# A two-block transformer on one core: the router's gate rows, count products, memsets and weight splits in another order

## The chip, the cores and the metric

The kernel runs on 1 core of one Trainium2 chip. The time is device microseconds from start to end of one execution; the figure for the kernel before is the median of 3 runs. The core has TensorE (PE, matrix products; PEld is its weight load), VectorE (DVE), ScalarE (ACT), GpSimd (POOL) and SyncE (SP, which here issues the weight loads). Each engine works through its own queue in order, and the queues wait for each other by semaphores.

## The reference

A block with feed-forward, recurrent, local and memory attention layers comes first; then two layers (0 and 1) of a second block. Each of these ends in a mixture of 16 experts for 256 tokens of width 1024. The change touches only this part:

```python
h = rmsnorm(x, norm2_g[l]) * (1.0 + sc2) + sh2
x = x + g2 * grouped_moe(h, w_router, router_bias, w_gate[l], w_up[l], w_down[l])
# grouped_moe: scores = sigmoid(t @ w_router); one group of 4 experts of 4 groups is chosen,
# in it the best 2 experts; their scores, normalised, weigh silu(t @ w_gate) * (t @ w_up) @ w_down
```

The modulation g2 (a row of 1024 numbers) multiplies the sum of the experts, and is needed on every partition.

## The kernel before, in words

All matrix products are made in three parts: a value is split into a high part and a low part (value minus high), and high x high, low x high and high x low are summed in PSUM (`PARTS`). For a weight tile (128 x 2048 numbers in a slot of a ring of 6 slots, loaded by SyncE) ScalarE makes the high part in two halves (`hi`, `split`, L706), and VectorE the low part, `w_lo`, in two halves (`lo`, `split`, L1928 and L1862). A tile's slot is loaded anew when TensorE has counted the tile as used.

Around the change a layer goes so. TensorE makes the products of the output projection, tiles w_out0 to w_out3 (L1111), and between them `gate_rows` (L1396): a product of a matrix of ones with the diagonal matrix of a modulation row, which puts the row on all partitions. VectorE makes the diagonal (`gate_diag`, L2050) and copies the result from PSUM (`gate_copy`, L2056). VectorE adds the projection to x (L2035, L2038), and the norm follows (L571 and L1782 to L1785). TensorE transposes the normed rows (`turn`, L1062), ScalarE and VectorE scale them on the way out of PSUM (L591, L1805). Then come a second `gate_rows`, for g2, the router's products (L1705), the sigmoid (L1035), and the selection on VectorE (L2509 to L2545), small steps of 0.2 us. Five products (L1712 to L1716) count for each expert the tokens ahead of each token, with `member`, the 0/1 matrix of the choice: the matrix `before` counts within a block of 128 tokens, `ones` gives the sum of a block. From the counts VectorE works out each token's slot and the matrix `pick` (L2561, L2564).

If every expert has at most 128 tokens, the branch `sparse` runs on every engine. TensorE gathers: 8 blocks k of 128 features for 512 slots, each into a PSUM bank (L1251, `gather`). ScalarE (L713, L715) and VectorE (L1935, L1936) turn each into a high and a low part, `xg_parts` (`expert_inputs`); semaphore `xg_act` counts ScalarE's, `xg_lo` VectorE's. Even blocks have their full value written by VectorE, odd ones by ScalarE. The columns behind slot 512 are set to 0 (L1987). Expert 0 then goes through its four tiles u0, g0, g1, u1 (up and gate, first and second half of the features; L1269); `weights` is a product that brings the slots' weights into a column of bank 4 (L1279), copied by VectorE (L1942). Behind u1 the slot numbers are spread over partitions (`spread`, L1324), and from expert 2 a loop runs over the experts. Every order named here is written out by hand.

## Time and profile before

| | us |
|---|---|
| median of 3 runs (1848.01 to 1850.01) | 1849.73 |
| the profiled execution | 1845.74 |
| its span, first to last instruction | 1843.9 |
| TensorE busy in it | 1668.1 (90%) |
| VectorE busy | 1230.0 (67%) |
| ScalarE busy | 1009.0 (55%) |
| mean granted TensorE clock | 0.955 |

Times in the rows further down are us from the span's start. A busy share is an average over stages: TensorE is full in the products, and idle in stretches such as the router's. The granted clock is 1.00 at TensorE's higher level (2.4 GHz) and 0.50 at its lower one (1.2 GHz).

### The profile page before, as it was taken

The numbers are of one execution on the slowest core, as the hardware profiler recorded it, in microseconds if no ns is written. First come the engines' busy times: TensorE is split into PE (matmuls) and PEld (weight loads), VectorE is DVE, ScalarE is ACT, GpSimd is POOL, SyncE is SP. The second block draws the span as 40 slices with busy tenths as digits, with TensorE's granted clock in tenths as the row PEclk, the third lists the DMA queues.
The fourth block names the chain that finished last, engine by engine and source line by source line (L and its number), as shares of the span: only waits on it lengthen the run. The fifth ranks groups of instructions, "written<-read, shape, count | busy, mean of one in ns | idle before, by whom it ended". The sixth has DMA issues, their size and how long they took to land.

```text
span 1843.9 us, 27068 instructions
## 1 busy us (share of the span) xinstructions
PE 1668.1 (90%) x10156; PEld 1428.9 (77%) x10156; DVE 1230.0 (67%) x1715; ACT 1009.0 (55%) x1407; POOL 27.0 (1%) x58
## 2 busy tenths in 40 slices
PE   6999997899998989876899999979897769999995
PEld 6999885488997968765688888869796657888884
DVE  5544355565546454764888888864677578888886
ACT  4444344253445433531788888844444258888884
POOL 2000000000000000001000000000000010000000
PEclk9999998999999999987899999999998879999998
DMA  8555478854554569722398998945431418898892
GB/s 261 186 188 190 144 246 269 277 167 160 183 188 145 165 207 348 274 91 92 133 331 315 333 330 313 333 144 163 137 116 68 137 63 297 320 333 319 329 333 89
DMA packets 245834, 401.86 MB, mean 218 GB/s; under 512 B 6522, under 2 KB 151596, under 8 KB 245756
## 3 DMA queue, kind: packets, MB, share of 16 engines
q1 hardware_dynamic: 244792, 398.77, 63.4%
q8 instruction: 55, 0.90, 0.2%
q0 software_dynamic: 592, 0.93, 0.2%
q10 hardware_dynamic: 372, 1.07, 0.2%
q14 instruction: 23, 0.19, 0.0%
HBM read 399.70 MB, written 1.05 MB: 217 GB/s over the span
## 4 chain that ended last, share of the span: by engine, by line
PE 80%; DVE 12%; ACT 4%; issue 2%; DMA 2%; DVEq 0%; ACTq 0%
PE bank L1269 19%; PE bank L1209 14%; PE bank L1293 10%; PE bank L1099 7%; PE bank L1222 6%; PE bank L1111 5%; PE bank L1087 5%; PE bank L1305 3%; PE bank L1136 2%; PE bank L1380 2%; DVE sb_w_lo L1862 2%; DMA sb_ring<-in_w_in 1%; PE bank L1556 1%; DVE sb_w_lo L1928 1%; PE bank L1125 1%
## 5 line engine op out<-in xcount | busy, mean ns | idle before, releaser
L1928 DVE TENSOR_TENSOR sb_w_lo<-sb_ring,sb_moe_hi 128x1024 fp32r<-128x1024 f32 x384 | 448.5, 1220 | 29.5 <-ACT sb_moe_hi L706 29.2
L706 ACT ACTIVATE sb_moe_hi<-sb_ring 128x1024 fp32r<-128x1024 f32 x384 | 381.8, 1058 | 69.2 <-PE bank L1293 33.7
L1883 DVE TENSOR_TENSOR sb_w_lo<-sb_ring,sb_w_hi 128x1024 fp32r<-128x1024 f32 x128 | 151.1, 1222 | 164.2 <-ACT sb_w_hi L661 163.9
L1209 PE MATMUL bank<-sb_hT_hi,sb_w_hi 128*128 128x256 f32 x704 | 201.3, 286 | 7.2 <-DVE sb_w_lo L1883 3.7
L661 ACT ACTIVATE sb_w_hi<-sb_ring 128x1024 fp32r<-128x1024 f32 x128 | 128.5, 1051 | 143.6 <-PE bank L1209 131.6
L1209 PE MATMUL bank<-sb_hT_lo,sb_w_hi 128*128 128x256 f32 x704 | 200.8, 285 | 0.0
L1209 PE MATMUL bank<-sb_hT_hi,sb_w_lo 128*128 128x256 f32 x704 | 200.7, 285 | 0.0
L1269 PE MATMUL bank<-sb_moe_hi,sb_xw_hi 128*128 128x512 f32 x480 | 193.6, 403 | 0.0
L1269 PE MATMUL bank<-sb_w_lo,sb_xw_hi 128*128 128x512 f32 x480 | 190.7, 397 | 0.0
L1269 PE MATMUL bank<-sb_moe_hi,sb_xw_lo 128*128 128x512 f32 x480 | 190.3, 397 | 0.0
L1862 DVE TENSOR_TENSOR sb_w_lo<-sb_ring,sb_proj_hi 128x1024 fp32r<-128x1024 f32 x100 | 117.9, 1221 | 92.0 <-ACT sb_proj_hi L641 91.9
L641 ACT ACTIVATE sb_proj_hi<-sb_ring 128x1024 fp32r<-128x1024 f32 x100 | 100.8, 1060 | 125.1 <-DMA sb_ring<-in_w_in 40.3
L1293 PE MATMUL bank<-sb_moe_hi,sb_hid_hi 128*128 128x512 f32 x512 | 145.4, 396 | 2.9 <-DVE sb_hid_hi L1954 2.9
L1209 PEld LDWEIGHTS bank<-sb_hT_hi,sb_w_hi 128*128 128x128 f32 x704 | 136.9, 194 | 8.6 <-DVE sb_w_lo L1883 4.1
L1209 PEld LDWEIGHTS bank<-sb_hT_lo,sb_w_hi 128*128 128x128 f32 x704 | 136.9, 194 | 0.7
L1209 PEld LDWEIGHTS bank<-sb_hT_hi,sb_w_lo 128*128 128x128 f32 x704 | 136.7, 194 | 0.0
L1099 PE MATMUL bank<-sb_w_lo,sb_hT_hi 128*128 128x256 f32 x480 | 136.0, 283 | 0.0
L1099 PE MATMUL bank<-sb_proj_hi,sb_hT_hi 128*128 128x256 f32 x416 | 119.8, 288 | 0.4 <-DVE sb_w_lo L1862 0.4
L1099 PE MATMUL bank<-sb_proj_hi,sb_hT_lo_l 128*128 128x256 f32 x416 | 117.9, 283 | 0.0
L1293 PEld LDWEIGHTS bank<-sb_moe_hi,sb_hid_hi 128*128 128x128 f32 x512 | 93.8, 188 | 21.3 <-DVE sb_hid_hi L1954 3.4
L1269 PEld LDWEIGHTS bank<-sb_moe_hi,sb_xw_lo 128*128 128x128 f32 x480 | 91.1, 190 | 21.7
L1269 PEld LDWEIGHTS bank<-sb_w_lo,sb_xw_hi 128*128 128x128 f32 x480 | 91.4, 190 | 20.0
(488 smaller groups left out, 3186.5 us busy)
## 6 DMA issues: line engine op xcount, KB each, us to landing
sb_ring<-in_w_up SPq DMA_DIRECT2D x64, 1024.0 KB, 5.3
sb_ring<-in_w_gate SPq DMA_DIRECT2D x64, 1024.0 KB, 5.3
sb_ring<-in_w_down SPq DMA_DIRECT2D x64, 1024.0 KB, 4.9
sb_ring<-in_ada_w SPq DMA_DIRECT2D x48, 1024.0 KB, 7.5
sb_ring<-in_w_in SPq DMA_DIRECT2D x46, 1024.0 KB, 5.4
sb_ring<-in_ffn_w_in SPq DMA_DIRECT2D x44, 1024.0 KB, 5.1
sb_ring<-in_ffn_w_out SPq DMA_DIRECT2D x22, 1024.0 KB, 4.9
sb_ring<-in_w_out SPq DMA_DIRECT2D x12, 1024.0 KB, 5.1
```

Source lines behind the costliest of these rows:

```text
L641: A(mix_hi(name)[:, c], ring[:, pos % RING, c], ACT.Copy).then_inc(s["mix_hi"], 1)
L661: A(w_hi[:, q % 2, c], ring[:, (pos0 + q) % RING, c], ACT.Copy).then_inc(s["w_hi"], 1)
L706: A(moe_hi[:, q % 3, c], ring[:, at % RING, c], ACT.Copy).then_inc(s["moe_hi"], 1)
L1087: ins = mm(out[:, j * SEQ:(j + 1) * SEQ], w[wp][:, k, j * P:(j + 1) * P], h_parts[hp][:, k, :], start=k == 0 and m == 0 and (turned is Non ...
L1099: ins = mm(out[:, t * FB:(t + 1) * FB], h_parts[hp][:, k, t * P:(t + 1) * P], w[wp][:, k, :], start=k == 0 and m == 0, stop=k == KC - 1 an ...
L1209: ins = mm(bank[4 + 2 * p + b][:, jj * SEQ:(jj + 1) * SEQ], w[wp][:, k, jj * P:(jj + 1) * P], h_parts[hp][:, k, :], start=k == 0 and m == ...
L1222: ins = mm(acc[2 * t + half][:, :], h, w[wp][:, kk, half * 512:(half + 1) * 512], start=start and kk == 0 and m == 0, stop=stop and kk == ...
L1269: ins = mm(out[:, :], x_parts[xp][:, 4 * kh + k, 0:P], w[wp][:, k, :], start=kh == 0 and k == 0 and m == 0, stop=kh == 1 and k == 3 and m ...
L1293: ins = mm(bank[6 + half][:, :], h[hp][:, 2 * kh + kk, :], w[wp][:, kk, half * 512:(half + 1) * 512], start=kh == 0 and kk == 0 and m == 0 ...
L1862: ins = tt(w_lo[:, pos % RING, c], ring[:, pos % RING, c], mix_hi(name)[:, c].bitcast(F32), ALU.subtract)
L1883: ins = tt(w_lo[:, slot, c], ring[:, slot, c], w_hi[:, q % 2, c].bitcast(F32), ALU.subtract)
L1928: ins = tt(w_lo[:, slot, c], ring[:, slot, c], moe_hi[:, q % 3, c].bitcast(F32), ALU.subtract)
```

## The change

The computation stays the same. Per layer of the second block:

- `gate_rows` for g2 goes from behind the transposes to ahead of them, behind the projection, into banks 0 and 1 in place of 4 and 5; it waits for the first half of x, which has been read out of these banks. Its diagonal goes ahead of w_out3's split on VectorE. The router's logits go to bank 2.
- The five count products become three, of 32, 32 and 16 columns; they now wait for the gate copy.
- The two memsets of `xg_parts` go from the start of `sparse` to ahead of the wait for the scores.
- ScalarE's splits of the first two expert tiles go from the start of `sparse` to behind the sigmoid.
- The gathered blocks 0 to 7 go to banks 4, 5, 0, 1, 2, 3, 6, 7 in place of 0 to 7.
- u0 waits for 4 input blocks in place of 6, `weights(0)` goes ahead of it, and on VectorE the split of g0 comes behind input 3, then the column's copy, then inputs 4 to 7.

```diff
+        IN_BANK = [bank[n] for n in (4, 5, 0, 1, 2, 3, 6, 7)]
...
-                hi(0)
-                hi(1)
                 expert_inputs()
...
-                A(rt[:, 0, :], bank[0][:, 0:T * NE], ACT.Sigmoid).then_inc(s["scores"], 1)
+                A(rt[:, 0, :], bank[2][:, 0:T * NE], ACT.Sigmoid).then_inc(s["scores"], 1)
+                for q in range(2):
+                    at = place[f"moe.{l}"] + q
+                    act.wait_ge(ring_full[at % RING], 16 * (at // RING + 1))
+                    for half in range(2):
+                        c = slice(half * TILE // 2, (half + 1) * TILE // 2)
+                        A(moe_hi[:, q, c], ring[:, at % RING, c], ACT.Copy).then_inc(s["moe_hi"], 1)
...
-                            ins = mm(bank[k][:, :], xn_parts[hl][:, t, k * P:(k + 1) * P], pick[:, t, 0:2 * SEQ],
+                            ins = mm(IN_BANK[k][:, :], xn_parts[hl][:, t, k * P:(k + 1) * P], pick[:, t, 0:2 * SEQ],
...
                 gather()
-                pe.wait_ge(s["xg_lo"], KC * l + 6)
+                pe.wait_ge(s["xg_lo"], KC * l + 4)
+                weights(0)
                 rows("u0", 0, bank[5], 0)
-                weights(0)
                 pe.wait_ge(s["w_slot"], NE * l + 1)
...
+                pe.wait_ge(s["x"], 7 + 4 * l)
+                gate_rows(2 * l + 2, bank[0:2])
                 turn(6 + 2 * l)
                 have_hT(6 + 2 * l)
-                gate_rows(2 * l + 2)
...
-                mm(bank[1][:, 0:NE], before, member[:, 0:NE], start=True, stop=True)
-                mm(bank[1][:, NE:2 * NE], before, member[:, NE:2 * NE], start=True, stop=False)
-                mm(bank[1][:, NE:2 * NE], ones[:, :], member[:, 0:NE], start=False, stop=True)
-                mm(bank[1][:, 2 * NE:3 * NE], ones[:, :], member[:, 0:NE], start=True, stop=False)
-                mm(bank[1][:, 2 * NE:3 * NE], ones[:, :], member[:, NE:2 * NE], start=False, stop=True)\
+                pe.wait_ge(s["gbc"], 2 * l + 2)
+                twice = member[:, 0:NE].unsqueeze(1).broadcast_to([P, 2, NE])
+                mm(bank[1][:, NE:3 * NE].rearrange("p (a e) -> p a e", a=2), ones[:, :], twice, start=True, stop=False,
+                   skip_group_check=True)
+                mm(bank[1][:, 0:2 * NE], before, member, start=False, stop=False, skip_group_check=True)
+                mm(bank[1][:, 2 * NE:3 * NE], ones[:, :], member[:, NE:2 * NE], start=False, stop=True, skip_group_check=True)\
...
-                for part in xg_parts:
-                    v.memset(part[:, :, 2 * SEQ:PICKS].bitcast(F32), 0.0)
                 lo(0)
-                for k in range(5):
+                for k in range(4):
                     expert_inputs(k)
                 lo(1)
-                for k in range(5, KC):
+                weights(0)
+                for k in range(4, KC):
                     expert_inputs(k)
-                weights(0)
                 lo(2)
+                lo(3)
                 cp(sel_r[0:NE, :, :], ident[0:NE, 0:NE].unsqueeze(2).broadcast_to([NE, NE, P])).then_inc(s["posT"], 1)
-                lo(3)
...
-                gate_copy(2 * l + 1, 0.5)
+                gate_copy(2 * l + 1, 0.5, bank[4:6])
+                gate_diag(l, 40)
                 split(f"w_out3.{l}")
...
                 normalise_x()
-                gate_diag(l, 40)
...
-                gate_copy(2 * l + 2, 1.0)
+                gate_copy(2 * l + 2, 1.0, bank[0:2])
+                for part in xg_parts:
+                    v.memset(part[:, :, 2 * SEQ:PICKS].bitcast(F32), 0.0)
```

On TensorE, layer 0, from the last projection product to the last count product, before (L1062 the transposes, L1396 the gate rows, L1705 the router, L1712 to L1716 the counts; `sb_dist` holds `member`, `sb_arena` the diagonal and `before`):

```order
L1111 MATMUL bank<-sb_proj_hi,sb_hT_lo_l 128x512 x2
L1062 MATMUL bank<-sb_ident,sb_xn 128x128 x16
L1396 MATMUL bank<-sb_arena,sb_ones 128x512 x2
L1705 MATMUL bank<-sb_router,sb_hT 128x16 x16
L1712 MATMUL bank<-sb_dist,sb_arena 128x16
L1713 MATMUL bank<-sb_dist,sb_arena 128x16
L1714 MATMUL bank<-sb_dist,sb_ones 128x16
L1715 MATMUL bank<-sb_dist,sb_ones 128x16
L1716 MATMUL bank<-sb_dist,sb_ones 128x16
```

and after (L1116, L1401, L1067, L1711, L1720 to L1723 are the same steps):

```order
L1116 MATMUL bank<-sb_proj_hi,sb_hT_lo_l 128x512 x2
L1401 MATMUL bank<-sb_arena,sb_ones 128x512 x2
L1067 MATMUL bank<-sb_ident,sb_xn 128x128 x16
L1711 MATMUL bank<-sb_router,sb_hT 128x16 x16
L1720 MATMUL bank<-sb_dist,sb_ones 128x32
L1722 MATMUL bank<-sb_dist,sb_arena 128x32
L1723 MATMUL bank<-sb_dist,sb_ones 128x16
```

The gate rows have moved ahead of the transposes, and two count products are gone.

On VectorE, layer 0, the split of w_out3 and what stands around it, before (L1862 a split, L2056 the gate copy, L2035 and L2038 the addition to x):

```order
L1862 TENSOR_TENSOR sb_w_lo<-sb_ring,sb_proj_hi 128x1024 x2
L2056 TENSOR_SCALAR sb_gbc<-bank 128x512 x2
L1862 TENSOR_TENSOR sb_w_lo<-sb_ring,sb_proj_hi 128x1024 x2
L2035 TENSOR_TENSOR sb_xn<-bank,sb_gbc 128x512 x2
L2038 TENSOR_TENSOR sb_x<-sb_x,sb_xn 128x1024
```

and after (L2054 is the diagonal):

```order
L1868 TENSOR_TENSOR sb_w_lo<-sb_ring,sb_proj_hi 128x1024 x2
L2060 TENSOR_SCALAR sb_gbc<-bank 128x512 x2
L2054 TENSOR_TENSOR sb_arena<-sb_ident,sb_modc 128x1024
L1868 TENSOR_TENSOR sb_w_lo<-sb_ring,sb_proj_hi 128x1024 x2
L2039 TENSOR_TENSOR sb_xn<-bank,sb_gbc 128x512 x2
L2042 TENSOR_TENSOR sb_x<-sb_x,sb_xn 128x1024
```

The diagonal now stands between the gate copy and the split.

On VectorE at the start of `sparse`, layer 0, before (L1987 the memsets, L1928 a weight split, L1935 and L1936 the expert inputs):

```order
L1987 MEMSET sb_xg_hi 128x8x128
L1987 MEMSET sb_xg_lo 128x8x128
L1928 TENSOR_TENSOR sb_w_lo<-sb_ring,sb_moe_hi 128x1024 x2
L1935 TENSOR_SCALAR sb_arena<-bank,sb_scol,sb_modc 128x512
L1936 TENSOR_TENSOR sb_xg_lo<-sb_arena,sb_xg_hi 128x512 x2
L1935 TENSOR_SCALAR sb_arena<-bank,sb_scol,sb_modc 128x512
L1936 TENSOR_TENSOR sb_xg_lo<-sb_arena,sb_xg_hi 128x512 x2
L1935 TENSOR_SCALAR sb_arena<-bank,sb_scol,sb_modc 128x512
L1936 TENSOR_TENSOR sb_xg_lo<-sb_arena,sb_xg_hi 128x512
L1928 TENSOR_TENSOR sb_w_lo<-sb_ring,sb_moe_hi 128x1024 x2
L1936 TENSOR_TENSOR sb_xg_lo<-sb_arena,sb_xg_hi 128x512
L1935 TENSOR_SCALAR sb_arena<-bank,sb_scol,sb_modc 128x512
```

and after (L1934, L1941, L1942 are the same steps, L1948 the column's copy):

```order
L1934 TENSOR_TENSOR sb_w_lo<-sb_ring,sb_moe_hi 128x1024 x2
L1941 TENSOR_SCALAR sb_arena<-bank,sb_scol,sb_modc 128x512
L1942 TENSOR_TENSOR sb_xg_lo<-sb_arena,sb_xg_hi 128x512 x2
L1941 TENSOR_SCALAR sb_arena<-bank,sb_scol,sb_modc 128x512
L1942 TENSOR_TENSOR sb_xg_lo<-sb_arena,sb_xg_hi 128x512 x2
L1934 TENSOR_TENSOR sb_w_lo<-sb_ring,sb_moe_hi 128x1024 x2
L1948 COPY sb_by_slot<-bank 128x1
L1941 TENSOR_SCALAR sb_arena<-bank,sb_scol,sb_modc 128x512
L1942 TENSOR_TENSOR sb_xg_lo<-sb_arena,sb_xg_hi 128x512 x2
L1941 TENSOR_SCALAR sb_arena<-bank,sb_scol,sb_modc 128x512
L1942 TENSOR_TENSOR sb_xg_lo<-sb_arena,sb_xg_hi 128x512 x2
L1934 TENSOR_TENSOR sb_w_lo<-sb_ring,sb_moe_hi 128x1024 x4
```

The memsets are gone from here, and the second split and the column's copy stand ahead of the last four inputs.

## Rows read from the trace of the kernel before

**Rows 1.** Windows of layer 0: length, busy us (instructions) per engine, PEclk, DMA, GB/s.

```profile
880.00:893.00 13.00, 9.39 (x33) 7.32 (x34) 12.62 (x16) 10.57 (x15) 0.00 (x0) 0.86 0.01 1
...
940.00:960.00 20.00, 20.00 (x93) 16.39 (x92) 17.46 (x19) 16.42 (x22) 0.00 (x0) 1.00 0.92 327
```

**Rows 2.** Timeline, layer 0, norm to router: start, us, engine, line, instructions, [idle before].

```profile
838.94 2.35 DVE L1862 TENSOR_TENSOR sb_w_lo<-sb_ring,sb_proj_hi 128x1024 fp32r<-128x1024 f32 x2
...
848.01 0.61 PE L1111 MATMUL bank<-sb_proj_hi,sb_hT_lo_l 128*128 128x512 f32 x2
...
854.64 1.22 DVE L2050 TENSOR_TENSOR sb_arena<-sb_ident,sb_modc 128x1024 f32<-128x1024 f32 x1
...
855.17 3.68 PE L1062 MATMUL bank<-sb_ident,sb_xn 128*128 128x128 f32 x16 [6.55 <-ACT sb_xn L578]
...
858.04 1.90 DVE L1805 TENSOR_SCALAR sb_hT<-bank,sb_scol,sb_modc 128x256 f32<-128x256 f32 x4 [2.18 <-PE bank L1062]
...
860.04 3.52 PE L1396 MATMUL bank<-sb_arena,sb_ones 128*128 128x512 f32 x4 [1.19 <-issue]
...
863.39 3.92 PE L1705 MATMUL bank<-sb_router,sb_hT 128*128 128x16 f32 x32
...
863.59 1.29 DVE L2056 TENSOR_SCALAR sb_gbc<-bank 128x512 f32<-128x512 f32 x2 [3.66 <-PE bank L1396]
867.35 0.20 ACT L1035 ACTIVATE sb_dist<-bank 128x32 f32<-128x32 f32 x1 [5.99 <-PE bank L1705]
```

**Rows 3.** Timeline, the router of layer 1.

```profile
1476.31 1.96 PE L1396 MATMUL bank<-sb_arena,sb_ones 128*128 128x512 f32 x4 [1.59 <-issue]
...
1478.10 4.19 PE L1705 MATMUL bank<-sb_router,sb_hT 128*128 128x16 f32 x32
...
1482.33 0.20 ACT L1035 ACTIVATE sb_dist<-bank 128x32 f32<-128x32 f32 x1 [4.70 <-PE bank L1705]
```

**Rows 4.** Windows of 1 us, TensorE: length, busy us (instructions), PEclk, DMA, GB/s.

```profile
863.00:864.00 1.00, 1.00 (x8) 0.91 0.00 0
...
866.00:867.00 1.00, 1.00 (x10) 0.80 0.00 0
...
883.00:884.00 1.00, 1.00 (x5) 0.67 0.00 0
...
893.00:894.00 1.00, 1.00 (x5) 0.95 0.00 0
...
1474.00:1475.00 1.00, 0.72 (x6) 0.91 0.00 0
```

**Rows 5.** Chain of waits, layer 0: start, us, engine, tile, line, number.

```profile
873.55 0.43 PE bank L1713 x2
...
892.78 4.55 PE bank L1269 x12
...
931.58 2.80 PE bank L1269 x12
```

**Rows 6.** Timeline, layer 0, gathering and first expert.

```profile
876.56 3.90 ACT L706 ACTIVATE sb_moe_hi<-sb_ring 128x1024 fp32r<-128x1024 f32 x4 [9.01 <-DVE sb_fits L2549]
...
879.84 1.22 PE L1251 MATMUL bank<-sb_pick,sb_xn_hi 128*128 128x512 f32 x2 [4.58 <-DVE sb_pick L2564]
880.11 0.91 DVE L1987 MEMSET sb_xg_hi<- 128x1024 f32 x1 [0.16 <-issue]
...
884.34 0.77 ACT L715 ACTIVATE sb_arena<-bank,sb_modc,sb_scol 128x512 f32<-128x512 f32 x1
...
888.56 0.61 PE L1251 MATMUL bank<-sb_pick,sb_xn_lo 128*128 128x512 f32 x2
...
889.77 2.35 DVE L1928 TENSOR_TENSOR sb_w_lo<-sb_ring,sb_moe_hi 128x1024 fp32r<-128x1024 f32 x2
...
892.78 0.50 PE L1269 MATMUL bank<-sb_moe_hi,sb_xg_hi 128*128 128x512 f32 x1 [3.61 <-DVE sb_xg_lo L1936]
...
906.63 1.21 PE L1324 MATMUL bank<-sb_posT,sb_sel_r 16*128 16x256 f32 x8
```

More of the change, by code:

```diff
@@ L382, in build @@
         SLOT_COUNTS = dict(
-            act=(("xg_act", KC), ("moe_hi", 12 * NE), ("xw", 2 * NE - 2), ("m_silu", NE), ("m_hid_hi", NE), ("ye_hi", NE), ("pos_out", NE // 2)),
+            act=(("xg_act", KC), ("moe_hi", 12 * NE - 4), ("xw", 2 * NE - 2), ("m_silu", NE), ("m_hid_hi", NE), ("ye_hi", NE), ("pos_out", NE // 2)),
             pe=(("gathered", KC), ("pos_turned", 1), ("pos_bc", NE // 2), ("w_psum", NE), ("m_hidT", NE), ("scattered", NE)),
@@ L712, in expert_inputs @@
                         put_in = dict(scale=scol[:, l, 1, k:k + 1], bias=modc[:, l, 24 + k:25 + k])
-                        ins = A(xg_parts[0][:, k, 0:2 * SEQ], bank[k][:, :], ACT.Identity, **put_in)
+                        ins = A(xg_parts[0][:, k, 0:2 * SEQ], IN_BANK[k][:, :], ACT.Identity, **put_in)
                         if k % 2:
-                            ins = A(xg_full[:, k, :], bank[k][:, :], ACT.Identity, **put_in)
+                            ins = A(xg_full[:, k, :], IN_BANK[k][:, :], ACT.Identity, **put_in)
                         ins.then_inc(s["xg_act"], 1)
@@ L1390, in ada_turn, with gate_rows @@
                 ins.then_inc(s["ada_turned"], 1)
-            def gate_rows(run):
+            def gate_rows(run, out):
                 pe.wait_ge(s["diag"], run)
                 for half in range(2):
-                    ins = mm(bank[4 + half][:, :], ones[:, :], diag[:, 4 * half:4 * half + 4, :], start=True, stop=True)
+                    ins = mm(out[half][:, :], ones[:, :], diag[:, 4 * half:4 * half + 4, :], start=True, stop=True)
                 ins.then_inc(s["gate_bc"], 1)
@@ L1696, in _ @@
                         pe.wait_ge(s["mT_dve"], 4 * l + 3)
-                        gate_rows(2 * l + 1)
+                        gate_rows(2 * l + 1, bank[4:6])
+                pe.wait_ge(s["x"], 7 + 4 * l)
+                gate_rows(2 * l + 2, bank[0:2])
                 turn(6 + 2 * l)
                 have_hT(6 + 2 * l)
-                gate_rows(2 * l + 2)
                 pe.wait_ge(s["router_in"], 32)
@@ L1704, in _ @@
                     for k in range(KC):
-                        ins = mm(bank[0][:, t * NE:(t + 1) * NE], hT[:, k, t * P:(t + 1) * P], router[:, k, :],
+                        ins = mm(bank[2][:, t * NE:(t + 1) * NE], hT[:, k, t * P:(t + 1) * P], router[:, k, :],
                                  start=k == 0, stop=k == KC - 1)
@@ L1719, in _ @@
                 pe.wait_ge(s["combine"], run)
-                pe.wait_ge(s["gbc"], 2 * l + 2)
                 fits_ = pe.value_load(fits[0:1, 0:1], min_val=0, max_val=1)
@@ L1934, in expert_inputs @@
                     if k % 2 == 0:
-                        link(ts(xg_full[:, k, :], bank[k][:, :], scol[:, l, 1, k:k + 1], modc[:, l, 24 + k:25 + k], M, AD))
+                        link(ts(xg_full[:, k, :], IN_BANK[k][:, :], scol[:, l, 1, k:k + 1], modc[:, l, 24 + k:25 + k], M, AD))
                     tt(xg_parts[1][:, k, 0:2 * SEQ], xg_full[:, k, :], xg_parts[0][:, k, 0:2 * SEQ].bitcast(F32), ALU.subtract)\
@@ L2051, in gate_diag, with gate_copy @@
                    modc[:, l, c0:c0 + KC].unsqueeze(2).broadcast_to([P, KC, P]), M).then_inc(s["diag"], 1)
-            def gate_copy(run, scale):
+            def gate_copy(run, scale, src):
                 v.wait_ge(s["gate_bc"], run)
                 for half in range(2):
-                    ins = ts(gbc[:, half * 512:(half + 1) * 512], bank[4 + half][:, :], scale, None, M)
+                    ins = ts(gbc[:, half * 512:(half + 1) * 512], src[half][:, :], scale, None, M)
                 ins.then_inc(s["gbc"], 1)
```

## Prediction

> **What bounds the kernel now.** I read the windows by stage first, then the timeline of one router and the first expert behind it, then the chain of waits through the same stretch. In the steady part of the experts TensorE is busy 20.00 of 20 us at a granted clock of 1.00 while the DMA engines are at 0.92 [rows 1]; the chain there is TensorE's own products, one tile of 12 after another in 2.80 us [rows 5]. So nothing that this change touches can be gained inside that loop: it is gained or lost ahead of it, and whatever moves the start of the first expert's products moves all that follows, in both layers, since the ring of weight tiles is refilled only as TensorE releases tiles. In the 13 us around the gathering of the tokens TensorE is busy 9.39 us, at a clock of 0.86 [rows 1]. That is the place: a serial chain norm, transposes, gate rows, logits, selection on VectorE, count products, gathering, first expert. The change works on five links of it, twice (layer 0 at 850 to 907 us, layer 1 at 1466 to 1522 us).
>
> **Gate rows (PE, L1396).** Today four passes stand between the transposes and the router's products. In layer 0 they start at 860.04 and the router follows at 863.39 to 863.55, so they cost 3.52 us there [rows 2]; in layer 1 from 1476.31 to 1478.10, 1.79 us [rows 3]. The factor of two is the clock: 512 columns in two passes at half speed, against full speed. After the change they stand behind the last product of w_out3, which ends at 848.62 [rows 2], and the first half of x, finished beside it; TensorE then idles until the transposes at 855.17, 6.5 us, so 1.8 us at the full clock are hidden. Their diagonal (1.22 us on DVE, L2050 [rows 2]) must be ready and now stands ahead of the last weight split. That split ran 838.94 to 841.29; shifted by 1.22 it ends at 842.5. The 24 products that need it end at 848.62 and take 24 x 0.233 = 5.6 us (12 in 2.80 us, [rows 5]), so they start at 843.0. It is hidden by 0.5 us; without that cover it would cost the overlap, at most 1.2 us in each layer. I take 0.
>
> But the gate rows also kept TensorE at work before the router. In layer 0 the clock is low through the transposes and rises only at 863.1, at the end of the gate rows; the router's 32 passes then run at full clock and it falls at 866.6 [rows 4]. They take 867.35 - 863.55 = 3.8 us with the last three or four low [rows 2]. In layer 1 it rose at 1474.1 during the transposes [rows 4], and the router took 4.2 us (1478.10 to 1482.33, [rows 3]), its last third low. A count pass, of the same shape but for a few columns, takes 0.43 / 2 = 0.215 us at the low clock [rows 5]; 32 such are 6.85 us. So if the clock stays low for the whole router, layer 0 ends at 860.04 + 6.85 = 866.9 instead of 867.35: +0.45 us gained, and layer 1 at 1483.15 instead of 1482.33: 0.8 us lost. If it is at full speed throughout (32 x 0.107 = 3.45 us), layer 0 gains 3.8 and layer 1 2.5 us. Without the gate rows nothing but the transposes precedes the router. They raised the clock in one layer and not in the other. I take the low end in layer 0 (+0.45) and the middle, rounded down, in layer 1 (+0.3): **0.75 us for both**, bounds -0.4 and +6.3.
>
> Here a rule stands against the middle. The row first: at 1474:1475 the clock is 0.91 although only transposes ran since 1465 [rows 4]. The Trainium skill (TensorE: Matmul & The Clock Gate, Part 4: PE-mode transpose) says that work in transpose mode does not count as busy for the clock and leaves it low. This trace disagrees in layer 1 and agrees in layer 0. By the rule both routers would be slow in the changed kernel, and this term -0.4 us in place of +0.75.
>
> **Count products.** Five products of two passes each, 0.43 us a product [rows 5], become three (two of 32 columns, one of 16; loading the weights, not the columns, sets the 0.215 us). Two products less are **0.86 us in each layer**. VectorE waits for them with nothing else left (its combine row is through by then). The wait for the gate copy, moved ahead of them, is met: in the new order that copy (1.29 us, [rows 2]) stands right behind VectorE's part of the transposes, which ends at 859.95, so it is done at 861.3, 11 us early.
>
> **Memsets.** Two of 0.91 us with 0.16 us of issue, 2.1 us per layer [rows 6], stand between selection and the first split on VectorE. In their new place they run 861.3 to 863.3, behind the gate copy and before the scores, which come at 867.35 today and between 863.8 and 867.2 afterwards. Hidden; if VectorE were late by all of it, 2 us a layer. ScalarE's four splits (3.90 us, [rows 6]) move from 876.56 to right behind the sigmoid, where it waited 9 us. They gain nothing by themselves: it is free at 880.46, before the first gathered block is there. What they buy is that the first split on VectorE has its data at once.
>
> **The first expert.** I count from the first gathering product (G = 879.84 in layer 0). Today [rows 6]: VectorE memsets until 2.2, split of u0 until 4.5, inputs 0 to 4, split of g0 at 9.93 to 12.2, input 5, and TensorE starts u0 at 12.94, 3.6 us after the last gathering product ended at 9.33. While it idled the clock went low again: it falls at 893.9 [rows 4], so the tile u0 took 4.55 us, not 2.80 [rows 5]. The spreading products start at 26.8 (906.63). There are two such stretches; layer 1's reads the same, 1494.82 to 1521.62, 26.8.
> The new order, with the same durations: split of u0 0.3 to 2.6; inputs 0 to 3 follow ScalarE, whose odd block 1 lands at 884.34 + 0.77, 5.3, and 2.0 us later block 3, at 7.3; block 3's low part is done at 8.0. Split of g0 8.0 to 10.3. TensorE ends the gathering at 9.33, does the weight column (0.41) and starts u0 at 9.75, at full clock since it never stopped: to 12.55; g0 to 15.35. On VectorE: column copy at 10.5, inputs 4 to 7 (two pairs of 2.05) to 14.6, split of g1 (2.3) to 16.85. That is late: **TensorE waits 1.5 us for the g1 split**, a new wait. g1 to 19.7, transposes of the slots 0.35, u1 (its split is done at 19.15) to 22.85, against 26.8. **3.95 us per layer, 7.9 for both.** Were no new wait there it would be 5.5 a layer; were the waiting to cost a stretch at low clock again (1.7 us, the excess of 4.55 over 2.80), 2.2. The other bank order only frees banks 4 and 5 first, which the column and u0 need; it costs nothing.
>
> **The gathering's clock.** It starts low in both layers, since nothing runs ahead of it, and rose after 3.8 us in layer 0 (at 883.66, [rows 4]) and 3.2 us in layer 1. When its start moves by some 1.3 us against the changes of the clock, the low stretch can be longer; each us of it costs 0.5. I take 1 us more in each layer, **-1.0 us for both**; bounds 0 and, all 32 passes low (13.7 us in place of 9.33), -4.4 a layer.
>
> **The sum.** 0.75 + 2 x 0.86 + 7.9 - 1.0 = 9.4 us, from the profiled execution's 1845.74 us (span 1843.9 and 1.8 around it) to 1836.4. The median of the runs is 1849.73, 4.0 above the profiled one, with the same work; I take the same difference off it: 1840.4 us.
>
> **Rivals.**
> (B) The clock pays back part: both routers low (-0.4) and the gathering's low stretch 3 us longer in each layer (-3.0). 1.7 + 7.9 - 3.4 = 6.2 us, 1843.5. For it: the two places where the change takes TensorE work away just before the router. Against it: the gathering itself is unchanged.
> (C) The clock is kind: routers at full speed (+6.3), gathering as now: 1.7 + 7.9 + 6.3 = 15.9 us, 1833.8. For it: layer 1 rose in the transposes. Against it: it fell within the router in both layers, and must then rise earlier than either.
> (D) The expert's gain goes into a new wait on VectorE. The column copy now stands before inputs 4 to 7, and waits for TensorE's column product, which waits for the gathering. If the gathering stays low to its end (13.7), the copy comes at 14.1, inputs to 18.4, g1 split 20.7, u1 ends at 26.6, the 26.8 of today. Left are the counts less the routers, 1.3 us: 1848.4. Against it: both layers rose at less than half of the gathering.
> (E) Slower: the same, and the low clock goes on through u0 and g0. It decides once the low stretch outlasts the gathering by both tiles: u0 and g0 take 5.1 us each, 14.1 + 10.2 = 24.3, then g1, transposes and u1 at full clock to 30.2, that is 3.4 us later than today per layer. -6.8 + 1.7 - 0.4 = -5.5, 1855.2. In its favour is only that u0 ran low in both layers today, but that followed 3.6 us of idling; here TensorE is busy without a gap.
> That the change does nothing is covered by D: the order of every queue does differ, and the steady loop can't take the time back, since TensorE sets it.
>
> **Chances.** Forecast 0.60, B 0.17, C 0.08, D 0.10, E 0.05. A measurement of this kernel can tell about 0.2%, 3.7 us, from no change. The forecast, B and C are beyond it: faster 0.85, D within it 0.10, E slower 0.05. The range, 1834.5 to 1846, holds the forecast with its bounds (2.2 instead of 3.95 in both experts gives 1843.9; full-clock routers in one layer about 1838), B and most of C, and leaves out D and E.
>
> **What would show it.** Right: gate rows at 848.7, seen in TensorE's timeline ahead of the transposes; the router's products directly behind them, whatever their clock; six count passes in 1.5 us; no memset behind the selection; 22 to 23.5 us from the first gathering product to the spreading ones, with a wait of 1 to 2 us for VectorE's split ahead of g1 and no low stretch in u0. Wrong: a wait ahead of w_out3's products for VectorE's split; scores found waiting because of the memsets; a low clock to the end of the gathering with VectorE idle at the column copy; or a tile of the steady loop longer than the 2.80 us of today [rows 5].

## The result, and the profile after

The changed kernel takes 1838.0 us (median of 4, 1835.05 to 1838.4) against 1849.87 (median of 4, 1848.01 to 1851.66) for the kernel before: a ratio of 0.9933, interval 0.9918 to 0.9948. Run once more, five times against nine, it takes 1839.42 against 1848.67, ratio 0.9948 (0.9934 to 0.9962). The gain is 9 to 12 us, where 9.4 was forecast. The profiled execution took 1837.8 us, its span 1836.1.

The timeline of the changed kernel, layer 0, from the projection's end to the counts (answers to [rows 2, 5]; L1401 gate rows, L1067 transposes, L1711 router, L2060 gate copy, L2505 memset, L1040 the early weight split, L1720 first count product):

```profile
848.08 1.98 PE L1401 MATMUL bank<-sb_arena,sb_ones 128*128 128x512 f32 x4
...
854.64 3.68 PE L1067 MATMUL bank<-sb_ident,sb_xn 128*128 128x128 f32 x16 [4.58 <-ACT sb_xn L579]
...
859.32 1.28 DVE L2060 TENSOR_SCALAR sb_gbc<-bank 128x512 f32<-128x512 f32 x2
...
859.50 6.98 PE L1711 MATMUL bank<-sb_router,sb_hT 128*128 128x16 f32 x32 [1.19 <-issue]
...
860.76 0.91 DVE L2505 MEMSET sb_xg_hi<- 128x1024 f32 x1 [0.16 <-issue]
...
866.52 0.20 ACT L1034 ACTIVATE sb_dist<-bank 128x32 f32<-128x32 f32 x1 [5.70 <-PE bank L1711]
866.61 3.88 ACT L1040 ACTIVATE sb_moe_hi<-sb_ring 128x1024 fp32r<-128x1024 f32 x4
...
872.12 0.63 PE L1720 MATMUL bank<-sb_dist,sb_ones 128*128 128x32 f32 x2 [5.63 <-DVE sb_dist L2546]
...
873.61 0.17 DVE L2554 TENSOR_REDUCE sb_dist<-bank 128x1 f32<-128x16 f32 x1 [0.68 <-PE bank L1723]
```

The gate rows run at 848.08, 1.98 us at the high clock, with the transposes 4.58 us of idling behind them. The router's products start 1.19 us behind the transposes, as nothing is between, but their 32 passes take 6.98 us; [rows 2] had 3.92. Gate copy and memsets lie within, 3.8 us clear of the scores. VectorE waits 0.68 us for the counts (1.53 before), which end 1.49 us after they start, against 2.36. Layer 1 is the same where [rows 3] had 4.19:

```profile
1472.56 6.98 PE L1711 MATMUL bank<-sb_router,sb_hT 128*128 128x16 f32 x32 [1.19 <-issue]
...
1479.57 0.20 ACT L1034 ACTIVATE sb_dist<-bank 128x32 f32<-128x32 f32 x1 [5.70 <-PE bank L1711]
```

The gathering and the first expert, layer 0 (answers to [rows 6]; L1256 gathering, L1934 a weight split, L716 ScalarE's block 1, L1284 the column product, L1948 its copy, L1274 expert tiles, L1329 the spreading):

```profile
878.16 1.22 PE L1256 MATMUL bank<-sb_pick,sb_xn_hi 128*128 128x512 f32 x2 [4.58 <-DVE sb_pick L2570]
878.18 2.36 DVE L1934 TENSOR_TENSOR sb_w_lo<-sb_ring,sb_moe_hi 128x1024 fp32r<-128x1024 f32 x2
...
882.66 0.77 ACT L716 ACTIVATE sb_arena<-bank,sb_modc,sb_scol 128x512 f32<-128x512 f32 x1
...
887.91 0.50 PE L1284 MATMUL bank<-sb_dist,sb_pick 128*128 128x1 f32 x4
...
888.27 0.49 PE L1274 MATMUL bank<-sb_moe_hi,sb_xg_hi 128*128 128x512 f32 x1
...
888.83 0.15 DVE L1948 COPY sb_by_slot<-bank 128x1 f32<-128x1 f32 x1
...
892.99 4.62 DVE L1934 TENSOR_TENSOR sb_w_lo<-sb_ring,sb_moe_hi 128x1024 fp32r<-128x1024 f32 x4
...
895.49 0.47 PE L1274 MATMUL bank<-sb_moe_hi,sb_xg_hi 128*128 128x512 f32 x1 [1.47 <-DVE sb_w_lo L1934]
...
901.39 1.21 PE L1329 MATMUL bank<-sb_posT,sb_sel_r 16*128 16x256 f32 x8
```

u0 starts 10.1 us after the first gathering product (12.94 before), right behind the column; g1 waits 1.47 us for the split (the wait ahead of 895.49); the spreading starts after 23.2 us, against 26.8.

Windows of 1 us, TensorE alone (length, busy us, PEclk, DMA, GB/s), answers to [rows 4]:

```profile
852.00:853.00 1.00, 0.00 (x0) 0.74 0.59 242
...
865.00:866.00 1.00, 1.00 (x6) 0.50 0.00 0
882.00:883.00 1.00, 1.00 (x3) 0.50 0.08 16
883.00:884.00 1.00, 1.00 (x5) 0.90 0.00 0
888.00:889.00 1.00, 1.00 (x8) 1.00 0.00 0
...
894.00:895.00 1.00, 0.02 (x1) 1.00 1.00 410
```

The clock stays low from 852.5 through the whole router and counts until 883.2, and is then high through u0 and the wait ahead of g1, where before it fell at 893.9. In layer 1 the wait ahead of g1 is 1.79 us, also at the high clock. Behind that stands one more wait, in the chain (start, us, what):

```profile
905.19 0.96 ACT sb_moe_hi L707
...
906.17 2.36 DVE sb_w_lo L1934 x2
908.53 0.61 DVE sb_hid_hi L1960
...
909.18 0.60 PE bank L1284 x4
...
926.16 2.80 PE bank L1274 x12
```

In the kernel before, u0 of expert 1 ran low in both layers (4.54 us). In layer 0 it now runs at the high clock, but the down products still wait for VectorE, which makes the low hidden part (L1960) only behind a weight split (L1934, waiting for ScalarE): of 1.7 us gained there only 0.3 arrives. In layer 1 the clock fell behind the spreading again and that tile took 4.55 us, so nothing was gained there. The tile of the steady loop is 2.80 us as before [rows 5].

**Where the time went**, from the profiles. Each stretch is the distance of starts: first transpose to sigmoid, counts to VectorE's maximum of them, first gathering product to the first product of down in expert 1; the last column is first transpose to that product, all stages in it:

| us, layer 0 / layer 1 | to sigmoid | counts | gathering to down | whole |
|---|---|---|---|---|
| before | 12.18 / 10.89 | 2.36 / 2.35 | 35.38 / 35.38 | 60.05 / 58.76 |
| before, again | 12.19 / 12.17 | 2.35 / 2.35 | 35.36 / 35.36 | 60.05 / 60.02 |
| after | 11.88 / 11.88 | 1.49 / 1.50 | 31.49 / 31.16 | 55.01 / 54.68 |
| after, again | 11.88 / 11.88 | 1.50 / 1.50 | 31.54 / 31.13 | 55.06 / 54.66 |
| gate rows alone | 11.88 / 11.88 | 2.35 / 2.35 | 35.16 / 36.81 | 59.52 / 61.18 |
| gate rows back | 12.18 / 12.18 | 1.50 / 1.50 | 31.45 / 31.39 | 55.26 / 55.21 |
| memsets back | 11.88 / 11.88 | 1.50 / 1.50 | 31.54 / 31.89 | 55.05 / 55.42 |
| order back | 11.88 / 11.88 | 1.50 / 1.50 | 36.56 / 36.44 | 60.08 / 59.94 |

Both stretches together: 118.81 before, 109.69 after, 9.12 us less; in the second pair of profiles 120.07 and 109.72, 10.35 less.

### The profile page after: what moved, and what is told of

It reads as the page before. It is cut to its first block, busy times and chain, and to the rows that moved or that the text cites. A ratio compares the mean times of both kernels' runs of the same rounds, so it can differ in the third digit from the quotient of the medians.

```text
span 1836.1 us, 27052 instructions
## 1 busy us (share of the span) xinstructions
PE 1670.2 (91%) x10148; PEld 1430.3 (78%) x10148; DVE 1230.2 (67%) x1715; ACT 1008.8 (55%) x1407; POOL 26.8 (1%) x58
## 4 chain that ended last, share of the span: by engine, by line
PE 80%; DVE 12%; ACT 4%; issue 2%; DMA 2%; DVEq 0%; ACTq 0%
PE bank L1274 19%; PE bank L1214 14%; PE bank L1298 10%; PE bank L1104 7%; PE bank L1227 6%; PE bank L1116 5%; PE bank L1092 5%; PE bank L1310 3%; PE bank L1141 2%; PE bank L1385 2%; DVE sb_w_lo L1868 2%; DMA sb_ring<-in_w_in 1%; PE bank L1561 1%; DVE sb_w_lo L1934 1%; PE bank L1130 1%
## 5 line engine op out<-in xcount | busy, mean ns | idle before, releaser
L1934 DVE TENSOR_TENSOR sb_w_lo<-sb_ring,sb_moe_hi 128x1024 fp32r<-128x1024 f32 x384 | 448.5, 1220 | 29.5 <-ACT sb_moe_hi L707 29.2
L707 ACT ACTIVATE sb_moe_hi<-sb_ring 128x1024 fp32r<-128x1024 f32 x376 | 373.7, 1058 | 42.0 <-PE bank L1298 33.4
L1274 PE MATMUL bank<-sb_moe_hi,sb_xw_hi 128*128 128x512 f32 x480 | 192.9, 402 | 0.0
L1274 PE MATMUL bank<-sb_w_lo,sb_xw_hi 128*128 128x512 f32 x480 | 190.1, 396 | 0.0
L1274 PE MATMUL bank<-sb_moe_hi,sb_xw_lo 128*128 128x512 f32 x480 | 189.9, 396 | 0.0
L1274 PEld LDWEIGHTS bank<-sb_moe_hi,sb_xw_lo 128*128 128x128 f32 x480 | 90.8, 189 | 21.5
L1274 PEld LDWEIGHTS bank<-sb_moe_hi,sb_xw_hi 128*128 128x128 f32 x480 | 90.8, 189 | 20.2 <-issue 0.2
```

The costliest lines, as they stand in the source:

```text
L707: A(moe_hi[:, q % 3, c], ring[:, at % RING, c], ACT.Copy).then_inc(s["moe_hi"], 1)
L1274: ins = mm(out[:, :], x_parts[xp][:, 4 * kh + k, 0:P], w[wp][:, k, :], start=kh == 0 and k == 0 and m == 0, stop=kh == 1 and k == 3 and m ...
L1934: ins = tt(w_lo[:, slot, c], ring[:, slot, c], moe_hi[:, q % 3, c].bitcast(F32), ALU.subtract)
```

## The experiments

**Gate rows alone, on the kernel before.**

```diff
-                turn(6 + 2 * l)
-                have_hT(6 + 2 * l)
-                gate_rows(2 * l + 2)
+                pe.wait_ge(s["x"], 7 + 4 * l)
+                gate_rows(2 * l + 2, bank[0:2])
+                turn(6 + 2 * l)
+                have_hT(6 + 2 * l)
...
                 gate_copy(2 * l + 1, 0.5, bank[4:6])
+                gate_diag(l, 40)
```

> The kernel before with one part of the change alone: the gate rows for g2 behind the last product of w_out3, into banks 0 and 1, their diagonal ahead of w_out3's split, the logits in bank 2, the wait for the gate copy ahead of the (five) count products. Theory: the router's 32 passes then run at the low clock, and the stretch from the first transpose to the sigmoid is 11.9 us in both layers, where it was 12.2 and 10.9; no gain, 1849 to 1850.5 us. Rival, from the run with the gate rows put back, which was 3.5 us above the changed kernel although its stretches were only 0.8 us longer: the part is worth about 3.5 us by some way that these stretches don't show, 1845 to 1847 us.

Measured: 1849.53 us (11 runs) against 1849.34 (15 runs), ratio 1.0002 (0.9993 to 1.0011). The router in layer 0 (timeline, TensorE and ScalarE):

```profile
860.49 6.98 PE L1706 MATMUL bank<-sb_router,sb_hT 128*128 128x16 f32 x32 [1.19 <-issue]
...
867.50 0.20 ACT L1035 ACTIVATE sb_dist<-bank 128x32 f32<-128x32 f32 x1 [5.69 <-PE bank L1706]
```

The stretch is 11.88 us in both layers, as expected: a part that takes 1.8 to 3.5 us of products off the path gives nothing. The rival falls. In layer 1 the low clock lasted until 5.6 us after the first gathering product and was low again through the whole of u0, and gathering to down grew to 36.81 us; in layer 0 it was 35.16.

**Gate rows back, in the changed kernel.**

```diff
-                pe.wait_ge(s["x"], 7 + 4 * l)
-                gate_rows(2 * l + 2, bank[0:2])
                 turn(6 + 2 * l)
                 have_hT(6 + 2 * l)
+                gate_rows(2 * l + 2, bank[0:2])
```

> The changed kernel with one part undone: the gate rows for g2 stand behind the transposes again, ahead of the router's products (still into banks 0 and 1; the diagonal stays early). Theory of the prediction: on their own the gate rows are worth 1.8 us at the high clock and 3.5 at the low one, but they also raise the clock for the router, so that the router's 32 passes take 3.4 to 4.2 us behind them and 7.0 without them, as measured in both layers of the changed kernel. Undoing the part should cost at most 1 us, or gain up to 1 us: 1837 to 1839 us beside 1838.0. Rival: the work moved off the path counts in full, 3.5 + 1.8 us or more, 1843 us or above. In the trace: the clock rises at the end of the gate rows or before, in at least one layer, and the stretch from the end of the transposes to the sigmoid is 8 us in both kernels within 1 us.

Measured: 1841.47 us (5 runs), ratio 0.9961 (0.9948 to 0.9973) to the kernel before, that is 2 to 3.5 us above the changed kernel. The stretch to the sigmoid grew by 0.30 in each layer, the whole by 0.25 and 0.53. Layer 1 (timeline):

```profile
1475.03 3.58 PE L1401 MATMUL bank<-sb_arena,sb_ones 128*128 128x512 f32 x4 [1.19 <-issue]
...
1478.45 3.86 PE L1710 MATMUL bank<-sb_router,sb_hT 128*128 128x16 f32 x32
...
1482.34 0.20 ACT L1034 ACTIVATE sb_dist<-bank 128x32 f32<-128x32 f32 x1 [5.99 <-PE bank L1710]
```

The router takes 3.86 us behind the gate rows' 3.58, 6.98 without them: the clock's part is as the theory has it. The time is above what was expected, and by the profiles most of it isn't in this place. Up to the first transpose, where both kernels have the same code, this execution was 1.06 us later than the changed kernel's first profile but 0.63 us earlier than its second, so that differs between executions of the same code. From layer 0's first down product to layer 1's first transpose, the same code too, it took 559.2 us, against 558.0 and 558.1, with the clock low for 39.6 us of it against 34.9. Whether the order of the gate rows brings that about is not shown; what the 2 to 3.5 us in the medians are beyond the 0.8 us of the stretches stays open.

**Memsets back.**

```diff
-                for part in xg_parts:
-                    v.memset(part[:, :, 2 * SEQ:PICKS].bitcast(F32), 0.0)
                 v.wait_ge(s["scores"], run)
...
+                for part in xg_parts:
+                    v.memset(part[:, :, 2 * SEQ:PICKS].bitcast(F32), 0.0)
                 lo(0)
```

> The changed kernel with the two memsets put back at the start of the sparse branch on VectorE, ahead of the split of u0. Theory: 2.1 us on VectorE there are mostly hidden, since input block 0 comes from ScalarE 2.9 us after the first gathering product and odd block 1 only at 5.3; the split of u0 would end at 4.5 in place of 2.4, inputs 0 to 3 catch up with ScalarE by block 3 (7.3), and u0 starts within 0.5 us of where it does now: 0 to 1.5 us in both layers together, 1838 to 1839.5 us. Rival: each us on VectorE in that stretch is a us on the path, as VectorE is what g1 waits for: 4.2 us, 1842 us.

Measured: 1838.84 us (5 runs), ratio 0.9947 (0.9934 to 0.9959). Timeline, layer 0 (L1993 memset, L1934 split of u0):

```profile
880.01 1.22 PE L1256 MATMUL bank<-sb_pick,sb_xn_hi 128*128 128x512 f32 x2 [4.58 <-DVE sb_pick L2570]
...
881.36 0.91 DVE L1993 MEMSET sb_xg_lo<- 128x1024 f32 x1 [0.16 <-issue]
...
882.19 2.29 DVE L1934 TENSOR_TENSOR sb_w_lo<-sb_ring,sb_moe_hi 128x1024 fp32r<-128x1024 f32 x2
...
897.43 0.47 PE L1274 MATMUL bank<-sb_moe_hi,sb_xg_hi 128*128 128x512 f32 x1 [1.51 <-DVE sb_w_lo L1934]
...
903.28 1.21 PE L1329 MATMUL bank<-sb_posT,sb_sel_r 16*128 16x256 f32 x8
```

The split of u0 ends 4.5 us after the first gathering product, as expected, and the spreading starts after 23.27, where it was 23.23. Layer 1 lost 0.7 us: there the gathering is a us shorter (8.94 us, not 9.96), TensorE reaches g1 sooner, and g1 starts 17.42 us after the first gathering product where it started at 16.67. The memsets' move is worth next to nothing in layer 0 and 0.7 us in layer 1, where VectorE is what TensorE waits for.

**Order of the first expert back.**

```diff
-                pe.wait_ge(s["xg_lo"], KC * l + 4)
-                weights(0)
+                pe.wait_ge(s["xg_lo"], KC * l + 6)
                 rows("u0", 0, bank[5], 0)
+                weights(0)
...
                 lo(0)
-                for k in range(4):
+                for k in range(5):
                     expert_inputs(k)
                 lo(1)
-                weights(0)
-                for k in range(4, KC):
+                for k in range(5, KC):
                     expert_inputs(k)
+                weights(0)
                 lo(2)
-                lo(3)
...
+                lo(3)
```

> The changed kernel with the order of expert 0 put back: u0 waits for 6 input blocks, the weight column behind u0, on VectorE the split of g0 behind input 4 and the column copy behind input 7, the slot patterns' copy ahead of the split of u1. Banks, memsets and ScalarE's splits stay moved. Theory: this order is the main term, nearly all of the 3.55 us from the first gathering product to the spreading ones in layer 0 and 4.25 in layer 1; undone, TensorE idles again between the gathering and u0 (2 to 3 us) and the clock falls in u0 or g0 (1.7 us): 1843 to 1845.5 us. Rival: the memsets and the early splits on ScalarE did it, and the order adds little: 1838 to 1840 us.

Measured: 1850.19 us (12 runs), ratio 1.0002 (0.9994 to 1.0011): the whole gain is gone, more than expected. The chain, layer 0:

```profile
892.98 5.49 PE bank L1274 x12
898.46 0.60 PE bank L1284 x4
...
899.30 3.03 PE bank L1274 x12
```

u0 starts 13.0 us after the gathering's start, as before, and takes 5.49 us, all of it low, where it took 4.55 [rows 5]. So this one edit is 5.1 and 5.3 us of the two stretches: 2.9 and 3.8 from the earlier u0 (1.0 of the 3.8 is the gathering itself, 9.90 us against 8.93, since its clock rose later), the rest where the clock is low in u0 and behind it; it stayed high when TensorE had no gap. The expectation was missed because it priced the order against the kernel before. With the order back, the low clock covers all of u0, and gathering to down takes 1.2 and 1.1 us longer than in the second profile of the kernel before; that takes back all that the count products (1.7 us) and the routers (0.6) still gain: 120.0 us for the two whole stretches, against 120.1. It also shows that the other bank order and the earlier splits on ScalarE give nothing without this order. Whether the order needs them was not tested; nor was the change of the count products undone by itself, its gain is read from the profiles.

**Idle products before the norm's transposes**, in the changed kernel; `busy(n)` makes n products whose result nobody reads.

```diff
+            def busy(n):
+
+                for _ in range(n):
+                    mm(bank[7][:, :], ones[:, :], diag[:, 0:4, :], start=True, stop=True)
...
                 gate_rows(2 * l + 2, bank[0:2])
+                busy(4)
                 turn(6 + 2 * l)
```

> The changed kernel with four idle products added on TensorE (ones with the diagonal, 512 columns, into bank 7, result unused) behind the gate rows, in the 4.1 us in which TensorE waits for the norm. They take 3.4 us at the high clock, so nothing waits for them. Theory: the router's products and the transposes are slow only because the clock is low after the idling; with the clock high until the router's end the transposes take 1.8 us less (about 1 us of it on the path) and the router's 32 passes 3.5 less: 3 to 4.5 us a layer, 1829 to 1832 us. If it falls within the router as in the kernel before, half of it: 1833 to 1835. Rival: the granted clock is not moved by such products, or the router's passes are bound by something else: 1838 us, no change.

Measured: 1833.95 us (5 runs), ratio 0.9921 (0.9908 to 0.9934). Timeline, layer 0 (L1400 the idle products):

```profile
849.49 3.60 PE L1400 MATMUL bank<-sb_arena,sb_ones 128*128 128x512 f32 x8
...
854.23 1.96 PE L1067 MATMUL bank<-sb_ident,sb_xn 128*128 128x128 f32 x16 [1.14 <-ACT sb_xn L579]
...
857.80 5.94 PE L1717 MATMUL bank<-sb_router,sb_hT 128*128 128x16 f32 x32 [1.60 <-ACT sb_hT L592]
...
863.77 0.20 ACT L1034 ACTIVATE sb_dist<-bank 128x32 f32<-128x32 f32 x1 [3.82 <-PE bank L1717]
```

The transposes take 1.96 us and not 3.68; the sigmoid comes 9.54 us (layer 0) and 8.23 us (layer 1) after the first transpose, not 11.88. The clock fell within the router in both layers, whose products took 5.94 and 4.62 us, not 6.98: over both layers about half of the router's loss came back, the second case of the expectation. It is the clock that makes the router slow, and products that do nothing move it.

**Idle products in three places.** Three more stand behind the router's products and three behind the count products.

```diff
+                busy(3)
                 pe.wait_ge(s["member"], run)
...
                     .then_inc(s["counts"], 1)
+                busy(3)
                 pe.wait_ge(s["fits"], run)
```

> The changed kernel with idle products (result unused) in three places on TensorE: four behind the gate rows as in the run before this, three behind the router while VectorE selects (5.6 us), and three behind the count products (4.5 us). Theory: with the clock high at the counts and the gathering, the counts take 0.6 us less, the gathering starts at full speed and u0 1 to 1.5 us sooner, on top of what four products before the norm gave: another 3 to 4 us in both layers, 1830 to 1831.5 us. Rival: where the clock is still low when they start, three products take 5.1 us in place of 2.6 and delay the gathering by 0.6 us, or the gathering is bound by ScalarE and not by its own speed: 1833 to 1835 us.

Measured: 1832.01 us (5 runs), ratio 0.9913 (0.9897 to 0.9929). The counts took 0.88 us where they took 1.5. Behind the last three products TensorE idled 1.9 us more; the gathering started at the high clock, which fell 1.1 us (layer 0) and 0.1 us (layer 1) after its first product and rose again at 4.5 and 3.5 us. u0 came after 9.4 us. The median is 1.9 us below the run before, between theory and rival; the two ratios' intervals overlap.

**Splits of the first two tiles in idle time.** ScalarE's go behind its split of w_out3, VectorE's low part of u0 behind that of w_out3 and of g0 behind the norm.

```diff
                 split(f"w_out3.{l}")
+                first_low(l, 0)
...
                 normalise_x()
+                first_low(l, 1)
...
-                lo(0)
-                for k in range(4):
-                    expert_inputs(k)
-                lo(1)
-                weights(0)
-                for k in range(4, KC):
+                for k in range(KC):
                     expert_inputs(k)
+                weights(0)
```

> The changed kernel with the splits of the first two expert tiles earlier still: ScalarE's behind its split of w_out3, VectorE's low part of u0 behind that of w_out3 and of g0 behind the norm, both in idle time; in the sparse branch VectorE goes from input to input, then the column's copy, then the split of g1. Theory: the wait ahead of g1 (1.5 us in layer 0, 2.0 in layer 1) comes from VectorE having 4.7 us of splits between inputs; without them g1 starts as soon as g0 ends, and nothing else is later: 3 to 4 us, 1834 to 1835.5 us. Rival: the inputs follow ScalarE's 2.0 us per pair, or the split of g1 waits for ScalarE's, which stands behind its inputs, so that g1 waits as long as now: 1837.5 to 1838.5 us.

Measured: 1835.82 us (5 runs), ratio 0.9935 (0.9919 to 0.9952), 2.2 to 3.6 us below the changed kernel and 0.3 us above the expected range. The chain, layer 0:

```profile
879.01 9.97 PE bank L1256 x32
888.98 0.34 PE bank L1284 x4
889.32 5.64 PE bank L1274 x24
```

Gathering, column, u0 and g0 (24 products, then g1) stand without a gap: the wait ahead of g1 is gone, and the spreading starts after 21.6 and 20.7 us, 1.7 and 1.9 sooner. In layer 1, 1.4 us of it was given back ahead of down, where u0 of expert 1 ran wholly at the low clock.

**Both together.**

> The early splits and the idle products in three places, together, in the changed kernel. Theory: they act on different links (VectorE in the first expert, TensorE's clock ahead of it), so the gains add: 1826 to 1828.5 us. Rival: with u0 sooner, the first expert is bound by ScalarE's inputs and by its split of g1, so most of one gain is lost in the other: 1830 us or above.

Measured: 1826.54 us (4 runs), ratio 0.9879 (0.986 to 0.9897). The gains add, within the expected range. By the profiles the two whole stretches together take 109.7 us in the changed kernel, 107.9 with the early splits, 102.5 with the idle products in three places and 100.7 with both: 1.8 and 7.2 us apart, 9.0 together.

**Five idle products behind the counts.** `busy(3)` there becomes `busy(5)`.

> Early splits and idle products as in the run before, with five in place of three behind the count products. With three, TensorE idled 1.9 us before the gathering, and the clock was low for the gathering's first 3.4 us in both layers. Theory: that last idling is what let it fall; five fill 4.3 of the 5.2 us at the high clock, the gathering runs at full speed from its start (8.0 us or less to u0, not 9.35) and 1.3 us a layer are gained: 1823.5 to 1824.5 us. Rival: ScalarE's pace of 2.0 us per pair of blocks, not the clock, ends the gathering's stretch, or the clock falls all the same: 1826 to 1827 us.

Measured: 1825.02 us (4 runs), ratio 0.9875 (0.9859 to 0.9892), the lowest of all, 0.5 us above the expected range; by the ratios not to be told from the run before. The mechanism is read from the profile, one execution with two layers (chain, layer 0; L1727 the first count product, L1256 the gathering):

```profile
870.39 0.41 PE bank L1727 x2
...
875.82 7.55 PE bank L1256 x32
883.37 0.34 PE bank L1284 x4
883.71 5.81 PE bank L1274 x24
```

All 32 gathering products at the high clock take 7.55 us (9.97 in the run with the early splits alone), u0 starts after 7.75 us in both layers, and the whole stretch is 47.85 / 47.61 us, against 50.08 / 50.61 with three. TensorE idled 0.2 us before the gathering, not 1.9. With three, the clock was high at the gathering's first product, unlike what the expectation says, and fell 1.2 and 0.15 us behind it. ScalarE's pace did not hold the gathering back, so the rival falls.

**The changed kernel and the kernel before, once more**, unaltered.

> The changed kernel once more, nothing altered. Its first median was 11.9 us below the kernel before, its profiled execution 7.9 below the other's, and the two stretches that the change touches are 9.1 us shorter in those profiles. Theory: the stretches are what the change does, and the rest is how the clock's low stretches fall elsewhere in the program in one execution or another: the median comes to 1839 to 1841 us. Rival: the change gains 12 us, 3 of them outside these stretches: 1837 to 1838.5 us.

Measured: 1839.42 us (5 runs) against 1848.67, as the theory had it; the first comparison's 1838.0 lies where the rival put it. The stretches of the two profiles of the changed kernel agree within 0.05 us.

> The kernel before once more, for a second profile. Theory: from the first transpose to the first down product it takes 58.8 to 61.5 us again in each layer, with the router's clock as the part that differs, and the time to the first transpose of layer 0 is 854.6 to 856.5 us, as in every run so far, whatever the kernel. Rival: the router's part is the same in every execution of this kernel (12.2 and 10.9 us to the sigmoid), set by the program.

Measured, one execution: 1850.75 us, span 1848.9. The router of layer 1 (timeline; gate rows, router, sigmoid):

```profile
1479.20 3.56 PE L1396 MATMUL bank<-sb_arena,sb_ones 128*128 128x512 f32 x4 [1.19 <-issue]
...
1482.59 3.87 PE L1705 MATMUL bank<-sb_router,sb_hT 128*128 128x16 f32 x32
...
1486.50 0.20 ACT L1035 ACTIVATE sb_dist<-bank 128x32 f32<-128x32 f32 x1 [5.98 <-PE bank L1705]
```

The gate rows took 3.56 us, not the 1.79 of [rows 3], and the sigmoid came 12.17 us after the first transpose, not 10.89. The rival falls: in this kernel the clock's level there changes from one execution to another. The first profile had caught layer 1 in the kinder case, by 1.3 us, and was with 1845.74 us one of the shortest executions of this kernel.

## Why the prediction was right

- **Gate rows, +0.75 us for both layers: mis-sized, -0.69 measured** (+0.30 and -0.99; against the second profile of before +0.31 and +0.29). The step that failed is the middle that I took for layer 1, 1.1 of the 1.4 us. The clock was low through the whole router in both layers of both profiles of the changed kernel, the low end of the range. With the gate rows gone from that place, neither the transposes nor the router's 32 products, 7 us without a gap, raised it. The other 0.3 us: from the router's start to the sigmoid I counted 6.85 us at the low clock, and it took 7.02 in layer 0 and 7.01 in layer 1. The Trainium skill's rule that I set aside (TensorE: Matmul & The Clock Gate, Part 4: PE-mode transpose) gave -0.4 and came closer in the first pair of profiles; against the second profile of before, the same two slow routers are a gain of 0.6 us. [Rows 4] still show one rise within transposes; in none of the other profiles without idle products did it come again, and I had given that one event half of the weight.
- **The diagonal** was hidden as said: w_out3's split ended at 841.9 in layer 0 of the new profile, and no wait stands ahead of its products.
- **Counts, 0.86 us a layer: 0.87 and 0.85.** The wait for the gate copy cost nothing.
- **Memsets and ScalarE's splits, hidden, 0:** the memsets were hidden in their new place, but in the old one they cost only 0.04 us in layer 0 and 0.74 in layer 1 of the 2.1 us that they take. ScalarE's splits were not undone by themselves.
- **First expert, 3.95 us a layer:** from the first gathering product to the spreading, 3.56 in layer 0 and 4.25 in layer 1. Without the gathering itself, which is the next term, that is 4.14 and 4.10. The new wait ahead of g1 was there with 1.47 and 1.79 us, where 1.5 was worked out. The spreading's start was worked out as 22.85 and came at 23.23 and 22.55.
- **The gathering's clock, -1.0 us:** in layer 0 it stayed low 5.0 us in place of 3.8 and the 32 products took 9.91 us in place of 9.33, 0.6 us lost within the figure above; in layer 1 they took 8.93 in place of 9.08, nothing lost. Counted together with the expert, gathering to down, 8.1 us were gained where 7.9 - 1.0 were forecast; the 1.2 us between come from this term (0.6), the expert (0.3) and the way from the spreading to down, which had no term (0.3).
- **The sum:** -0.69 + 1.72 + 8.11 = 9.1 us in the first pair of profiles, forecast 9.4. Two errors of opposite sign, of 1.4 and 1.2 us, cancelled: that the total came so close is luck, that the expert's order is its main term is not. The medians, 11.9 and 9.3 us apart in two comparisons, lie on either side of the forecast. The profiled spans differ by 7.8 only: 0.5 us were gained ahead of the first transpose, where the code is the same, and 1.8 lost between layer 0's first down product and layer 1's first transpose, where the clock of the changed kernel's execution was low for 34.9 us against 28.0, once more at 1296 to 1300 among others. In the second pair the spans differ by 11.0.
- **Rivals.** B had its first half (both routers low), C did not happen, D and E neither. The range was said to hold most of C, but C's own value, 1833.8, lies outside it. The run with the idle products shows what lay behind D and E: what TensorE does ahead of the gathering decides its speed; without the idle products the clock rose within 5.6 us of the gathering's first product in every profile here, less than half of the 13.7 us of low clock that D needs.

## What to carry to other kernels

Work moved off a serial path gives back only what the work behind it does not lose: products just ahead of a chain of small ones also keep TensorE's clock up, so price the stretch, not the item. In such a chain count what VectorE does between the inputs that TensorE waits for, and move splits whose data are there early into a stretch where VectorE and ScalarE idle. Where TensorE must idle on a serial path before work that matters, products without a use in that idle time can pay: here 4 to 5.5 us of 1838 before the transposes alone, and with products in three places and the early splits 13 to 14 us in all. That is shown for this kernel alone.

## What was not expected

- Idle products raised the speed of everything behind them: transposes 3.68 to 1.96 us, the counts 1.5 to 0.88, the gathering 9.97 to 7.55. The kernel with them, and with more work, is the fastest, 1825.0 us against 1838 to 1839.4.
- With three idle products behind the counts TensorE idled 1.9 us before the gathering, and the clock fell within the gathering's first 1.2 us in both layers of both profiles; with five it idled 0.2 us, and the clock was not low there at all.
- The router's products at the high clock (32 passes in 3.9 us) did not keep it there: it fell within them in every profile in which it was high at their start.
